# A two-block transformer layer on one core: POOL's matrix powers paced by tiles of the first feed-forward, products of ones at a boundary, and the output stored in quarters

## The chip, the cores and the metric

One core of a Trainium2 chip runs the whole program in one launch. The metric is the device time of the execution in microseconds (us); lower is better. The core has TensorE (PE, matrix products, with its weight loads as PEld), VectorE (DVE), ScalarE (ACT), GpSimd (POOL) and SyncE (SP, which here only issues transfers). The engines run their own instruction streams and meet at semaphores: `wait_ge(s, n)` holds an engine until semaphore `s` has reached `n`.

## The reference

256 tokens of width 1024 in float32 go through nine stages, each of which adds to the tokens `x`:

```python
x = x + 0.5 * ga1 * rms_norm(swiglu(modulate(rms_norm(x), sh1, sc1)))   # ffn 0
x = x + ga2 * rms_norm(mixer_1(modulate(rms_norm(x), sh2, sc2)))        # mix1: window attention + S5
x = x + 0.5 * ga3 * rms_norm(swiglu(modulate(rms_norm(x), sh3, sc3)))   # ffn 1
x = x + 0.5 * swiglu(rms_norm(x))                                       # ffn 2
x = x + mixer_2(rms_norm(x))                                            # mix2
x = x + 0.5 * swiglu(rms_norm(x))                                       # ffn 3, ffn 4
x = x + mixer_3(rms_norm(x))                                            # mix3
x = x + 0.5 * swiglu(rms_norm(x))                                       # ffn 5
out = rms_norm(x)
```

A feed-forward is `silu(h @ w_gate) * (h @ w_up)) @ w_down` with a hidden width of 2816, that is 22 tiles of 128. The modulation (`sh`, `sc`, `ga`) is `silu(c) @ w_ada + b_ada`, a product of one row with a 1024 x 9216 matrix. The S5 part of mix1 is a complex linear recurrence, `state = lam_bar * state + B_bar u`, `y = Re(C state)`. The kernel computes it in steps of four tokens and needs for that the powers of `lam_bar` multiplied into `B` and into `C`, turned into matrices for TensorE: the input map, the near map (what tokens of one step do to each other) and the output map. They depend on the parameters alone, so they are prepared during ffn 0.

## The kernel before

**Float32 by three products.** Every float32 operand of a large product is split into `hi` (rounded to the fast float32r form, by ScalarE) and `lo` (the rest, by VectorE), and `product3` (line 202) makes hi*hi + hi*lo + lo*hi: three passes through TensorE.

**The stream of panels.** All weights come as 458 panels of 128 x 1024. SP loads a panel into one of six `raw` buffers, ScalarE makes `w_hi` of it (`split_hi`, line 179), VectorE `w_lo` (`split_lo`, line 187), TensorE uses it and counts `panel_used`, which frees the buffer. So the splits can run at most six panels ahead of the products.

**A feed-forward.** Tile f has three panels: gate, up and down. `ffn_pe` (line 507) runs `up(f)` (gate and up products, 48 matmuls) and then `down(f - 1)` (12 wider ones), because between `up(f)` and `down(f)` ScalarE makes the silu, VectorE the hidden product (line 668, counted in `hidden_done`), ScalarE `f_hi` and VectorE `f_lo` (line 673). ScalarE and VectorE take, in their own programs, the three panel splits of group f, then the hidden work of tile f. `tiles(lo, hi)` is a loop over pairs of tiles: `tiles(0, 4)` is tiles 2 to 9.

**What else happens in ffn 0.** VectorE adds up the modulation: 2.5 additions of 128 x 1024 a tile (line 843), whose panels SP loads as well; at the end of the stage (tiles 18 to 21) TensorE sums the columns and the gate, and VectorE finishes them (lines 917 to 934). POOL works through `tables_pool` (line 1086): it issues three loads, computes four powers of B and four of C (`times_complex`, line 1072: six operations of 128 x 256 each), then two double angles, and then waits until `map_evacuated` has reached OUTPUT_MAP to build the table of rotations, `rot`, in the same memory as the powers of C. ScalarE widens and evacuates the maps: `input_wide_act` (needs `powers_ready` 1, after the B powers; eight activations), `near_map_act`, `input_map_act` twice, `output_map_act` (needs `powers_ready` 2; four activations). TensorE makes the products of the near map between its tiles and transposes the input map in two parts (`input_map_pe`, line 1183). All evacuations count one semaphore, `map_evacuated`, and every wait on it names a total. So the totals follow the order in which ScalarE does them:

```python
INPUT_WIDE, NEAR_MAP, INPUT_MAP, OUTPUT_MAP = 8, 9, 17, 21     # line 990
pe.wait_ge(map_evacuated, NEAR_MAP + max(n - 1, 0))            # line 1187, before transposes n = 0..7
pool.wait_ge(map_evacuated, OUTPUT_MAP)                        # line 1121, before the rotations
```

**Boundaries.** After a stage VectorE adds the four quarters of the result to X (a quarter is 128 tokens x 512 channels; quarters 0 and 2 come first into a "plain" stage), TensorE transposes X by 128 x 128 tiles (`turn_pe`, line 422), ScalarE and VectorE make `h_hi` and `h_lo` of them, and `norm_pe` (line 453) runs the first products of the next stage k tile by k tile. Stages from index PLAIN = 3 (ffn 2 is the first) scale by the norm only later. The boundary into ffn 2 is the only one into a plain stage behind a stage that is normed itself: VectorE multiplies the result by the gate row (line 764, counted in `times_gate`) before it adds (line 772), and there is no product left over for `last_quarter`. `keep_busy` (line 428) makes products of a matrix of ones, whose result nobody reads; some other boundaries have them.

**The end.** `norm_pool` makes the reciprocal root for each half of the tokens, VectorE multiplies each half (line 2830, 128 x 1024) and POOL stores each half (line 2774).

## Time and profile before

| | us |
|---|---|
| three runs: median (lowest to highest) | 1576.78 (1573.79 to 1578.28) |
| the profiled execution | 1575.49 |
| its span in the profile | 1573.7 |
| mean granted TensorE clock, as a share of full speed | 0.993 |
| ffn 0 on TensorE, from its first product to its last | 37.4 to 255.4 |
| boundary into ffn 2 | about 593 to 609 |
| last multiplication starts | 1566.3 |

All times of the trace are from the start of the span. A row of a time line is: start, duration, engine, line, operation, output and input by the program's names, count of instructions merged, and in brackets the idle time before it with what ended it. A row of the windows is: stretch, its length, then for each engine busy time and instruction count, then PEclk (the clock granted to TensorE; 1.00 is 2.4 GHz and 0.50 is 1.2 GHz), the busy share of the 16 DMA engines, and GB/s. Matmuls are pipelined, so neighbouring records overlap.

### The profile page before, as it was taken

The page shows a single profiled execution, that of the slowest core. Times are in us where ns is not written, and L with a number is a line of the kernel's source. Part 1 is how long each engine was busy: PE and PEld are TensorE (multiplying, and loading weights), DVE is VectorE, ACT ScalarE, POOL GpSimd, SP SyncE. Part 2 cuts the span into 40 slices and gives each one's busy share as a digit, 9 for nine tenths or more (in the row PEclk, how much of TensorE's full clock was granted, in tenths as well). Part 3 has the DMA queues.
Part 4 walks back from the last instruction along what each step waited for, and adds up shares of the span by engine and source line. Part 5 has one row for each costly group of instructions (what it writes and reads, how often), then busy time and mean ns, then how long its engine had stood idle before and what let it go on. Part 6 is the DMA issues. An engine that isn't in the chain of part 4 may idle for free.

```text
span 1573.7 us, 28410 instructions
## 1 busy us (share of the span) xinstructions
PE 1524.4 (97%) x10512; PEld 1401.8 (89%) x10512; DVE 1023.6 (65%) x1391; ACT 758.5 (48%) x1205; POOL 222.7 (14%) x255
## 2 busy tenths in 40 slices
PE   5989999999999998999999999999999999999997
PEld 5989999989988888999997899999999999899996
DVE  6998778766665456655567765556655569565554
ACT  2444645576456345444454344445444457454442
POOL 1596095311001011000000000000000000000000
PEclk9999999999999999999999999999999999999999
DMA  9888874236665455655543365554655544255551
GB/s 349 320 299 279 315 266 130 79 108 199 203 224 186 168 188 209 225 189 175 196 132 96 110 227 170 194 185 136 212 188 189 174 156 137 68 200 191 171 198 40
DMA packets 80563, 294.35 MB, mean 187 GB/s; under 512 B 9051, under 2 KB 9404, under 8 KB 79916
## 3 DMA queue, kind: packets, MB, share of 16 engines
q1 hardware_dynamic: 75728, 274.97, 50.8%
q0 software_dynamic: 3984, 16.21, 3.1%
q10 hardware_dynamic: 780, 2.18, 0.5%
q8 instruction: 50, 0.82, 0.2%
q14 instruction: 21, 0.17, 0.0%
HBM read 289.13 MB, written 3.15 MB: 186 GB/s over the span
## 4 chain that ended last, share of the span: by engine, by line
PE 84%; DVE 8%; ACT 3%; issue 2%; DMA 1%; POOL 1%; SPq 0%; DVEq 0%; ACTq 0%
PE bank L207 74%; DVE w_lo L191 3%; DVE arena L843 2%; PE bank L431 1%; PE bank L2033 1%; PE bank L2022 1%; PE bank L1273 1%; DMA arena<-ada 1%; PE bank L2409 1%; PE bank L2387 1%; ACT arena L308 1%; PE bank L424 1%; ACT w_hi L185 0%; PE bank L1259 0%; POOL stat L349 0%
## 5 line engine op out<-in xcount | busy, mean ns | idle before, releaser
L207 PE MATMUL bank<-h_hi,w_hi 128*128 128x256 f32 x2344 | 674.4, 288 | 5.8 <-DVE w_lo L191 4.4
L207 PE MATMUL bank<-h_lo,w_hi 128*128 128x256 f32 x2344 | 664.7, 284 | 0.0
L207 PE MATMUL bank<-h_hi,w_lo 128*128 128x256 f32 x2344 | 664.5, 283 | 0.0
L191 DVE TENSOR_TENSOR w_lo<-raw,w_hi 128x1024 fp32r<-128x1024 f32 x454 | 548.4, 1257 | 109.0 <-ACT w_hi L185 108.3
L185 ACT ACTIVATE w_hi<-raw 128x1024 fp32r<-128x1024 f32 x458 | 457.9, 1050 | 55.0 <-DMA raw<-panels 28.8
L207 PEld LDWEIGHTS bank<-h_hi,w_hi 128*128 128x128 f32 x2344 | 450.7, 192 | 21.0 <-issue 6.8
L207 PEld LDWEIGHTS bank<-h_lo,w_hi 128*128 128x128 f32 x2344 | 450.9, 192 | 5.7 <-issue 1.9
L207 PEld LDWEIGHTS bank<-h_hi,w_lo 128*128 128x128 f32 x2344 | 450.7, 192 | 0.0
L668 DVE TENSOR_TENSOR arena<-arena,bank 128x256 f32<-128x256 f32 x132 | 55.3, 419 | 253.7 <-PE bank L207 180.7
L207 PE MATMUL bank<-w_hi,f_hi 128*128 128x512 f32 x528 | 207.8, 394 | 1.6 <-DVE f_lo L673 1.4
L207 PE MATMUL bank<-w_hi,f_lo 128*128 128x512 f32 x528 | 206.9, 392 | 0.0
L207 PE MATMUL bank<-w_lo,f_hi 128*128 128x512 f32 x528 | 205.6, 389 | 0.0
L606 ACT ACTIVATE f_hi<-arena 128x256 fp32r<-128x256 f32 x132 | 55.1, 418 | 256.7 <-DVE arena L668 256.7
L348 POOL TENSOR_SCALAR stat<-stat 128x1 f32<-128x1 f32 x26 | 11.8, 455 | 995.3 <-ACT arena L308 994.5
L600 ACT ACTIVATE arena<-arena 128x256 f32<-128x256 f32 x88 | 36.8, 418 | 196.1 <-DVE arena L662 196.1
L207 PEld LDWEIGHTS bank<-w_lo,f_hi 128*128 128x128 f32 x528 | 99.2, 188 | 21.7
L207 PEld LDWEIGHTS bank<-w_hi,f_hi 128*128 128x128 f32 x528 | 99.6, 189 | 19.4 <-issue 1.6
L207 PEld LDWEIGHTS bank<-w_hi,f_lo 128*128 128x128 f32 x528 | 99.7, 189 | 15.8
L843 DVE SCALAR_TENSOR_TENSOR arena<-arena,stat 128x1024 f32<-128x1024 f32 x70 | 96.1, 1374 | 2.5 <-DMA arena<-ada 1.1
L673 DVE TENSOR_TENSOR f_lo<-arena,f_hi 128x256 fp32r<-128x256 f32 x132 | 60.9, 461 | 50.8 <-ACT f_hi L606 50.8
L604 ACT ACTIVATE arena<-bank 128x256 f32<-128x256 f32 x44 | 16.8, 382 | 134.1 <-PE bank L207 134.1
L662 DVE TENSOR_TENSOR arena<-bank,arena 128x256 f32<-128x256 f32 x88 | 37.2, 423 | 20.4 <-PE bank L207 20.4
(329 smaller groups left out, 1387.2 us busy)
## 6 DMA issues: line engine op xcount, KB each, us to landing
raw<-panels SPq DMA_DIRECT2D x458, 512.0 KB, 4.6
arena<-ada SPq DMA_DIRECT2D x64, 512.0 KB, 5.2
arena<-ada POOLq DMA_DIRECT2D x8, 512.0 KB, 3.9
arena<-rows POOLq DMA_DIRECT2D x4, 512.0 KB, 4.6
spectrum<-arena POOLq DMA_DIRECT2D x2, 1024.0 KB, 7.9
arena<-spectrum POOLq DMA_DIRECT2D x1, 2048.0 KB, 18.0
X<-x_in SPq DMA_DIRECT2D x1, 1024.0 KB, 6.7
arena<-decay ACTq DMA_DIRECT2D x2, 512.0 KB, 5.6
```

The costliest lines, as they stand in the source:

```text
L185: act.activation(w_hi[:, slot, :], raw[:, slot, :], ACT.Copy).then_inc(hi_ready, 1)
L191: dve.tensor_tensor(w_lo[:, slot, :], raw[:, slot, :], w_hi[:, slot, :].bitcast(F32), ALU.subtract).then_inc(lo_ready, 1)
L207: last = pe.matmul(out_ap, a, b, start=start and n == 0, stop=stop and n == 2)
L308: return act.activation(squares[:, q, :], source, ACT.Square, scale=D ** -0.5, accum_out=stat[:, at + q:at + q + 1])
L424: tr = pe.transpose(turned_out(n, k)[:, m * P:(m + 1) * P], X[:, m, k * P:(k + 1) * P], ident[:, :])
L600: act.activation(ffn_buf[:, f % 2, :], gate_buf[:, f % 2, :], ACT.Silu).then_inc(silu_done, 1)
L604: act.activation(ffn_buf[:, f % 2, :], gate_out(at, f), ACT.Silu).then_inc(silu_done, 1)
L606: act.activation(f_hi[:, f % 2, :], ffn_buf[:, 2 + f % 2, :], ACT.Copy).then_inc(f_hi_done, 1)
L662: dve.tensor_tensor(gate_buf[:, f % 2, :], gate_out(at, f), rstd_row[:, :], ALU.mult).then_inc(gate_scaled, 1)
L668: dve.tensor_tensor(ffn_buf[:, 2 + f % 2, :], ffn_buf[:, f % 2, :], up_out(at, f), ALU.mult).then_inc(hidden_done, 1)
L673: dve.tensor_tensor(f_lo[:, f % 2, :], ffn_buf[:, 2 + f % 2, :], f_hi[:, f % 2, :].bitcast(F32), ALU.subtract).then_inc(f_lo_done, 1)
L843: dve.scalar_tensor_tensor(out=dst, in0=src, scalar=c, in1=dst, op0=ALU.mult, op1=ALU.add).then_inc(ada_used, 1)
```

## The change

POOL computes the double angles before the powers, and every power but the first waits for a count of hidden products of ffn 0. ScalarE and TensorE take up the maps one pair of tiles later; the output map now comes ahead of the input map's evacuations, and the totals of `map_evacuated` are renumbered to fit. At the boundary into ffn 2 TensorE makes 14 products of ones before the transposes and, once all four gated quarters have been read, 5 more after the first eight transposes. The final multiplication is done in quarters, and SP stores three of them and ScalarE the last, in place of POOL's two halves.

```diff
@@ norm_pe
             if plain(n):
+                if n == PLAIN:
+                    keep_busy(pe, 7, 14)
                 for m in range(MT):
                     pe.wait_ge(x_done, added(n, 0, m))
                     for k in range(4):
                         turn_pe(pe, n, k, m)
+                if n == PLAIN:
+                    pe.wait_ge(times_gate, 4 * n)
+                    keep_busy(pe, 1, 5)
                 if n - 1 >= PLAIN:
                     last_quarter(pe, n - 1)
@@ ffn_pe, n == 0
-                tiles(0, 4)
+                tiles(0, 5)
                 near_map_first_pe(pe)
-                up(10, between=lambda: near_map_pe(pe, 0, 4))
+                up(12, between=lambda: near_map_pe(pe, 0, 4))
                 near_map_pe(pe, 4, 8)
-                down(9)
+                down(11)
                 near_map_pe(pe, 8, 12)
-                up(11, between=lambda: near_map_pe(pe, 12, STATE_TILES))
-                down(10)
-                tiles(5, 6)
+                up(13, between=lambda: near_map_pe(pe, 12, STATE_TILES))
+                down(12)
+                tiles(6, 7)
                 input_map_pe(pe, 0)
-                tiles(6, 7)
+                tiles(7, KT)
                 input_map_pe(pe, 1)
-                tiles(7, KT)
                 up(2 * KT + 2)
@@ ffn_act, n == 0
-                tiles(0, 3)
+                tiles(0, 4)
                 input_wide_act(act)
-                tiles(3, 5)
+                tiles(4, 6)
                 near_map_act(act)
-                tiles(5, 6)
+                tiles(6, 7)
+                output_map_act(act)
                 input_map_act(act, 0)
-                tiles(6, 7)
+                tiles(7, KT)
                 input_map_act(act, 1)
-                output_map_act(act)
-                tiles(7, FT // 2 - 2)
+                tiles(KT, FT // 2 - 2)
@@
-        INPUT_WIDE, NEAR_MAP, INPUT_MAP, OUTPUT_MAP = 8, 9, 17, 21
+        INPUT_WIDE, NEAR_MAP, OUTPUT_MAP, INPUT_MAP = 8, 9, 13, 21
@@ tables_pool: the block of the powers moves behind the double angles
             c1, s1 = double_angle(pr(LR), pr(LI))
             c1, s1 = double_angle(pr(YI), pr(EM1))
+            pool.wait_ge(ssm_loaded, 32)
+            raw_r, raw_i, c_r, c_i = [by_channel(ssm_raw[:, j, :]) for j in range(4)]
+            times_complex(pool, order, power_of(b_powers, 0, 3), power_of(b_powers, 1, 3), raw_r, raw_i,
+                          pr(CR), pr(CI))
+            for j in (2, 1, 0):
+                pool.wait_ge(hidden_done, 8 - 2 * j)
+                times_complex(pool, order, power_of(b_powers, 0, j), power_of(b_powers, 1, j),
+                              power_of(b_powers, 0, j + 1), power_of(b_powers, 1, j + 1), pr(DT), pr(XR))
+            pool.sem_inc(powers_ready, 1)
+            for i in range(STEP):
+                pool.wait_ge(hidden_done, (10, 12, 13, 14)[i])
+                source = (c_r, c_i) if i == 0 else (power_of(c_powers, 0, i - 1), power_of(c_powers, 1, i - 1))
+                times_complex(pool, order, power_of(c_powers, 0, i), power_of(c_powers, 1, i), *source,
+                              pr(DT), pr(XR))
+            pool.sem_inc(powers_ready, 1)
+
             pool.wait_ge(map_evacuated, OUTPUT_MAP)
@@ input_map_pe
-                pe.wait_ge(map_evacuated, NEAR_MAP + max(n - 1, 0))
+                pe.wait_ge(map_evacuated, OUTPUT_MAP + max(n - 1, 0))
@@ the end
+        def store_final(eng, q):
+            m, half = q // 2, quarter(q)
+            eng.wait_ge(final_done, q + 1)
+            eng.dma_start(out[m * P:(m + 1) * P, half], final[:, m, half]).then_inc(out_stored, 16)
@@ sync, behind the last load_panel
+            for q in (0, 1, 2):
+                store_final(sp, q)
+            sp.wait_ge(out_stored, 64)
@@ gpsimd
-            for m in range(MT):
-                pool.wait_ge(final_done, m + 1)
-                pool.dma_start(out[m * P:(m + 1) * P, :], final[:, m, :]).then_inc(out_stored, 16)
-            pool.wait_ge(out_stored, 32)
@@ scalar, behind the last norm_act
+            store_final(act, 3)
@@ vector
-            for m in range(MT):
+            for q in range(4):
+                m, half = q // 2, quarter(q)
                 dve.wait_ge(rstd_done, 2 * last + m + 1)
-                dve.scalar_tensor_tensor(out=final[:, m, :], in0=X[:, m, :],
-                                         scalar=stat[:, RS + m:RS + m + 1], in1=final_row[:, :],
+                dve.scalar_tensor_tensor(out=final[:, m, half], in0=X[:, m, half],
+                                         scalar=stat[:, RS + m:RS + m + 1], in1=final_row[:, half],
                                          op0=ALU.mult, op1=ALU.mult).then_inc(final_done, 1)
```

## Rows read from the trace of the kernel before

**Rows 1.** The page: shares of the chain that ended last, by engine.
```profile
PE 84%; DVE 8%; ACT 3%; issue 2%; DMA 1%; POOL 1%; SPq 0%; DVEq 0%; ACTq 0%
```

**Rows 2.** Groups of VectorE, 65 to 135 us: shapes, count | busy us, mean ns | idle before.
```profile
L191 DVE TENSOR_TENSOR w_lo<-raw,w_hi 128x1024 fp32r<-128x1024 f32 x21 | 33.5, 1647 | 2.0 <-ACT w_hi L185 2.0
L843 DVE SCALAR_TENSOR_TENSOR arena<-arena,stat 128x1024 f32<-128x1024 f32 x19 | 28.6, 1506 | 0.1
L673 DVE TENSOR_TENSOR f_lo<-arena,f_hi 128x256 fp32r<-128x256 f32 x7 | 6.4, 911 | 0.0
```

**Rows 3.** The same groups of VectorE, 146 to 196 us.
```profile
L843 DVE SCALAR_TENSOR_TENSOR arena<-arena,stat 128x1024 f32<-128x1024 f32 x13 | 16.6, 1279 | 0.1
L191 DVE TENSOR_TENSOR w_lo<-raw,w_hi 128x1024 fp32r<-128x1024 f32 x12 | 14.0, 1218 | 4.2 <-ACT w_hi L185 4.2
...
L673 DVE TENSOR_TENSOR f_lo<-arena,f_hi 128x256 fp32r<-128x256 f32 x5 | 2.1, 417 | 0.0
```

**Rows 4.** Time line of POOL: first and last of 48 power operations, then the rotations' start.
```profile
65.73 0.89 POOL L1075 TENSOR_TENSOR arena<-arena,par 128x256 f32<-128x256 f32 x1 [2.60 <-DMA arena<-skip]
...
133.02 1.60 POOL L1080 TENSOR_TENSOR arena<-arena 128x256 f32<-128x256 f32 x1
...
196.84 0.96 POOL L938 MEMSET arena<- 128x1024 f32 x1 [52.22 <-ACT arena L1149]
```

**Rows 5.** The chain that ended last, one undisturbed feed-forward tile: start, duration, count.
```profile
499.31 8.50 PE bank L207 x60
```

**Rows 6.** Time line of TensorE around the gap in feed-forward 0.
```profile
114.51 0.39 PE L207 MATMUL bank<-w_lo,f_hi 128*128 128x512 f32 x1
118.13 0.39 PE L207 MATMUL bank<-h_hi,w_hi 128*128 128x256 f32 x1 [3.23 <-DVE w_lo L191]
```

**Rows 7.** Windows of 2 us before and after that gap.
```profile
96.00:98.00 2.00, 0.84 (x6) 0.67 (x6) 2.00 (x2) 0.00 (x0) 1.84 (x3) 1.00 0.80 219
...
118.00:120.00 2.00, 1.87 (x12) 1.87 (x13) 2.00 (x3) 0.98 (x2) 2.00 (x2) 0.76 0.60 172
120.00:122.00 2.00, 2.00 (x11) 2.00 (x11) 2.00 (x3) 0.43 (x2) 1.92 (x3) 0.50 0.80 248
```

**Rows 8.** Time line of ScalarE: input widening, f_hi of tile 15, output widening.
```profile
110.01 5.86 ACT L1149 ACTIVATE arena<-arena,C 128x1024 f32<-128x1024 f32 x8
...
187.98 0.42 ACT L606 ACTIVATE f_hi<-arena 128x256 fp32r<-128x256 f32 x1 [0.65 <-DVE arena L668]
...
192.46 4.26 ACT L1149 ACTIVATE arena<-arena,C 128x1024 f32<-128x1024 f32 x4
```

**Rows 9.** Time line of TensorE: the input map's second transposes, behind tile 15.
```profile
189.50 1.03 PE L1189 MATMUL bank<-ident,arena 128*128 128x128 f32 x8
```

**Rows 10.** Windows at the boundary into ffn 2, and one 230 us earlier.
```profile
597.00:600.00 3.00, 1.99 (x9) 1.99 (x10) 3.00 (x6) 2.45 (x8) 0.00 (x0) 0.50 0.03 5
600.00:603.00 3.00, 3.00 (x16) 3.00 (x16) 1.23 (x3) 0.95 (x2) 0.00 (x0) 0.50 0.42 143
...
368.00:370.00 2.00, 2.00 (x17) 1.88 (x17) 2.00 (x5) 1.39 (x5) 1.37 (x3) 1.00 0.00 0
```

**Rows 11.** Time line of TensorE at the boundary into ffn 2.
```profile
594.61 0.66 PE L424 MATMUL bank<-ident,X 128*128 128x128 f32 x4 [1.48 <-DVE X L772]
596.30 0.65 PE L424 MATMUL bank<-ident,X 128*128 128x128 f32 x4 [1.03 <-DVE X L772]
598.01 0.58 PE L207 MATMUL bank<-h_hi,w_hi 128*128 128x256 f32 x1 [1.06 <-DVE h_lo L407]
```

**Rows 12.** Time line of TensorE: 24 calls of `keep_busy` at the boundary into ffn 1.
```profile
368.50 5.52 PE L431 MATMUL bank<-ones 128*128 128x128 f32 x48
```

**Rows 13.** Time line of the end: last multiplication and POOL's issue of its store.
```profile
1566.28 1.28 DVE L2830 SCALAR_TENSOR_TENSOR arena<-X,stat,arena 128x1024 f32<-128x1024 f32 x1 [0.84 <-POOL stat L349]
1567.87 0.53 POOL L2774 DMA_DIRECT2D out<-arena  x1 [1.04 <-DVE arena L2830]
```

**Rows 14.** Transfers by issue: engine, count, KB each, us from issue to landing.
```profile
out<-arena POOLq DMA_DIRECT2D x2, 512.0 KB, 2.9
```

More of the change, by code:

```diff
@@ L1094, in tables_pool @@
             order(pool.tensor_copy(pr(XR), pr(LI)))
-            pool.wait_ge(ssm_loaded, 32)
-            raw_r, raw_i, c_r, c_i = [by_channel(ssm_raw[:, j, :]) for j in range(4)]
-            times_complex(pool, order, power_of(b_powers, 0, 3), power_of(b_powers, 1, 3), raw_r, raw_i,
-                          pr(CR), pr(CI))
-            for j in (2, 1, 0):
-                times_complex(pool, order, power_of(b_powers, 0, j), power_of(b_powers, 1, j),
-                              power_of(b_powers, 0, j + 1), power_of(b_powers, 1, j + 1), pr(DT), pr(XR))
-            pool.sem_inc(powers_ready, 1)
-            for i in range(STEP):
-                source = (c_r, c_i) if i == 0 else (power_of(c_powers, 0, i - 1), power_of(c_powers, 1, i - 1))
-                times_complex(pool, order, power_of(c_powers, 0, i), power_of(c_powers, 1, i), *source,
-                              pr(DT), pr(XR))
-            pool.sem_inc(powers_ready, 1)
             c1, s1 = pr(COS), pr(SIN)
```

## The prediction

> **What bounds the kernel now.** I read the shares of the page first: TensorE carries 84% of the chain that ended last, VectorE 8% and ScalarE 3% [rows 1]. So nearly every microsecond is a product, and the change can only touch the few places where the products stop. Next I read the time lines of the engines around the three edits. Three places matter.
>
> First, tiles 3 to 9 of feed-forward 0 (of 22). A tile of a feed-forward takes TensorE 8.5 us when it waits for nothing [rows 5]. Per tile VectorE has three panel subtractions, a hidden product, f_lo and 2.5 additions of the modulation sums. Where POOL is computing its powers these cost 1.65, 1.51 and 0.91 us [rows 2], where it rests 1.22, 1.28 and 0.42 us [rows 3]. With the overlap of neighbouring records taken off, a tile is 9.6 us for VectorE with POOL at work (3 x 1.6 + 0.4 + 0.9 + 2.5 x 1.4) and 7.2 without. POOL's powers run without a break from 65.7 to 134.6 us [rows 4], so there VectorE, at 9.6 us against TensorE's 8.5, sets the pace and falls behind. When ScalarE then widens the input map for 5.9 us [rows 8], nothing is left in store, and TensorE stands from 114.9 to 118.1 us [rows 6], released by a w_lo. Right after that gap its granted clock falls to the lower of the two levels, 1.2 GHz: 0.76 and 0.50 of 2.4 GHz in the next windows of 2 us [rows 7].
>
> Second, the boundary into the third feed-forward. TensorE ends its products at 593.1 (1.48 us of idle time before 594.61), makes transposes at 594.6 and 596.3 and gets its first product at 598.0 [rows 11]; from 597 to past 603 the clock stands at 0.50 [rows 10].
>
> Third, the end: the last multiplication starts at 1566.28, POOL issues its store at 1567.87 [rows 13], it lands 2.9 us after its issue [rows 14], and 2.9 us more pass until the span ends at 1573.7.
>
> **Part 1, the paced powers.** The double angles move ahead of the powers: 134.6 to 144.6 us is 10.0 us of POOL [rows 4], so powers start at about 73.2 instead of 65.7. One power is 68.9 / 8 = 8.6 us [rows 4]. The new waits hold the second to fourth b power to tiles 3, 5 and 7, the c powers to tiles 9, 11, 12 and 13. up(9) starts at 118.1 now [rows 6] and, with what is found below, at about 113; at 8.5 us a tile [rows 5] this puts the hidden products of tiles 3, 5 and 7 at about 70, 88 and 105.5, tile 9's at 123, and tile 15's at about 180, the near map's products being in between. So b runs at 73 to 82, 82 to 91 (tile 3 is long done), 91 to 100, then a rest until tile 7 at about 105.5, 106 to 115, and c at 123 to 131, 141 to 150, 151 to 160, 162 to 171. Everything queued behind them on POOL waits too: the two increments that ScalarE needs. The first comes at 115, wanted after tile 9; the second at 171, wanted after tile 15. Neither is late.
>
> VectorE is then slowed about half of the time between 66 and 123 instead of all of it. It loses 2.4 us a tile under POOL, so 23 us over 9.6 tiles become about 14, and it was TensorE's 8.5 that it had to meet: the panels are no longer late at tiles 6 to 8. What goes at most is the gap of 3.2 us [rows 6], the loss at the low clock, 2 x 0.24 + 2 x 0.50 = 1.5 us and 0.2 until it is back [rows 7], the 1.2 us without a product at 96 to 98 us (0.84 busy of 2.00 [rows 7]) and 0.3 of gaps too small for a row: 6.4 us. What is late next is the same widening of the maps, now after tile 9. Between the end of up(9) and the start of up(11) TensorE has 11.3 us of work (down, up, down: 2.75 + 5.75 + 2.75, which are 8.5 us and a third of it more [rows 5]); the path through tile 9's hidden product, its f_hi, 5.9 us of widening, one w_hi and one contended w_lo takes 9.3 us and VectorE's own lateness. That lateness I get as about 3.4 us (it loses 1.1 us a tile under POOL, and wins 1.3 in between), so 1.4 us of a gap stay. Part: 6.4 - 1.4 = **-5.0 us**; ends -6.4 and -1.4 (VectorE as late as now).
>
> **The wait that the change adds.** In the new numbering the evacuations are 8 input wide, 9 near map, 13 output map, 21 input map, and `input_map_pe` starts with a wait for 13: the transposes of the input map stand behind all four widenings of the output map, for no reason of data. Today those widenings come after everything (192.46) and nobody on TensorE waits for them. In the changed order ScalarE is through with a tile's f_hi 1.1 us before TensorE reaches the transposes (187.98 + 0.42 = 188.4 against 189.5 [rows 8, 9]) and then widens for 4.3 us [rows 8]: 188.4 + 4.3 - 189.5 = 3.2 us in which TensorE stands, and behind it everything else in its program. ScalarE's near map, the contention of the last c power and a late hidden product can make it 4.3. I take **+3.5**; ends 0 (were the vector engines' panels late there anyway) and +4.3. A gap of 3.2 us has cost the clock in this very stage [rows 6, 7], so I add its **+1.7**; ends 0 and +3.1 (half of the 6.2 us at 0.50 of the boundary [rows 10]). The Trainium skill ("TensorE: Matmul & The Clock Gate", Part 4) says that transposes do not count as activity for the clock; the 16 transposes of the map would then lengthen the quiet stretch, and the trace agrees so far as eight transposes at 594.6 and 596.3 did not hold the clock [rows 10, 11]. By that rule the fall is certain, by row 6 alone it is likely.
>
> The rotation, which waits for the output map, starts about 11 us earlier (186 instead of 196.84 [rows 4]) and ends at 237 instead of 248. Its longest operations then lie on VectorE's sums for the second gate (229 to 235 today) and no longer on the last two tiles. I take **+0.3**; ends -1.0 and +1.8 (the sums slowed as in rows 2). Part 1 together: -5.0 + 3.5 + 1.7 + 0.3 = **+0.5 us**.
>
> **Part 2, products of ones.** 24 such calls are 48 instructions in 5.5 us [rows 12], 0.115 us each. 14 calls: 28 x 0.115 = 3.2 us, from 593.1 to 596.3. The first transposes could have gone at 594.6; they go at 596.3 and end at 596.7, and the second ones, ready at 596.3, are 0.4 us late; the path runs through these. 5 calls, 1.15 us, fill 597.2 to 598.3 while h_hi and h_lo are made. The new wait for the gated quarters holds nothing: VectorE gates the last of them before the addition that releases the second transposes. The products of the first k tiles, 598.0 to 603.4, then run at 2.4 GHz instead of 1.2: 5.4 / 2 = 2.7 us less. The squares and the row of reciprocals follow the last of these tiles, so they move along. -2.7 + 0.4 and 0.1 for a step of the h_lo chain that becomes the slower one = **-2.2 us**; ends -2.7 and +0.4 (the clock falls all the same).
>
> **Part 3, the store.** The last quarter is ready when the last half is today, plus 0.1 us for the start of one more instruction. Its issue need not wait 0.3 us for POOL (1566.28 + 1.28 against 1567.87 [rows 13]), and it moves 256 KB instead of 512, which saves between nothing and half of 2.9 us [rows 14]; I take 0.6, in the lower half, since it still has 128 rows to place. Three of four stores go behind SP's last panel load and one behind ScalarE's last square; nothing is queued behind them. -0.3 - 0.6 + 0.1 = -0.8, and a little of the 0.53 us that POOL's issue itself takes [rows 13]: **-0.9**; ends +0.1 and -1.8. The Trainium skill ("DMA: Bandwidth & Descriptors", Latency and other measured facts) gives a first byte after 0.6 us on the hardware queues and 1 us on POOL's; by that the part would be 0.4 us more of a gain. No row here shows it.
>
> **Sum**: +0.5 - 2.2 - 0.9 = -2.6 us. The profiled execution took 1575.49 us (span 1573.7 and 1.8 around it), 1.3 below the median of the three runs, 1576.78. 1575.5 - 2.6 = 1572.9; against the median 1574.2, which I give, as the runs after will be judged so. About 0.3% (4.7 us) can be told from no change.
>
> **The rivals.**
> A. The map wait costs no clock and VectorE really gets ahead: part 1 is -6.4 + 3.2 + 0 - 0 = -3.2, the sum -6.3, 1570.5 us. For it: the fall needs a gap, and a ScalarE that is early makes it shorter. Against: the gap before the fall today is as long [rows 6]. 0.25.
> B. The products of ones do not hold the clock at the boundary: part 2 is +0.4, the sum 0.0, 1576.8 us. For it: they are the same 128 columns wide as the transposes. Against: at the boundary before, 24 calls [rows 12] hold 1.00 [rows 10]. 0.12.
> C, slower. VectorE stays the bound of tiles 3 to 9, so that only 1.4 us of the early loss go, and the transposes of the input map wait 4.3 us and lose 3.1 us of clock, with the gate's sums slowed by 1.8: -1.4 + 4.3 + 3.1 + 1.8 = +7.8, less 3.1 of the other parts, +4.7 us, 1581.5. It decides from a lateness of 5.3 us of the hidden product of tile 9 after up(9), where the gap is again 3.2 us. For it: three b powers still run without a break. Against: the rests before tiles 7 and 9. 0.10.
> D. The edit does nothing at that place, since the powers' contention is only moved: early gain 3 instead of 5, sum -0.6, 1576.2. 0.08.
>
> **How the numbers follow.** The forecast, 0.45, reaches from 1571.5 to 1577. Faster by over 0.3% are A and a small part of the forecast: 0.32. Slower is C and nothing else: 0.10. The rest, 0.58, is within 0.3%. The range takes in A and B and stops short of C: 1569.0 to 1579.0.
>
> **What would show it.** Right: in the stretch from 75 to 123 us no TensorE gap over 2 us and the clock at 1.00; powers in six bursts; a TensorE gap of 3 to 4.5 us before L1189's first transposes, released by ScalarE's L1149, and a clock of 0.5 in the 5 us after it; the boundary near 595 at 1.00 with the row product about 2 us sooner after the last down product; the last store landing within 2.5 us. Wrong: a gap of the old size at the widening (C), no gap at the transposes (A), a 0.50 near 600 (B).

## The result, and the profile after

| | before | after |
|---|---|---|
| median of 6 runs on one chip, us | 1575.34 (1573.03 to 1578.28) | 1566.87 (1566.01 to 1568.16) |
| profiled execution, us | 1575.49 | 1566.55 |
| its span, us | 1573.7 | 1563.9 |
| mean granted clock | 0.993 | 0.997 |

The changed kernel takes 0.9946 of the time of the kernel before, 95% interval 0.9932 to 0.9960: 8.5 us less. The forecast was 2.6 us less and its range ended at 1569.0, so the result lies outside it, on the fast side. Of the 7.3 us between the forecast of 1574.2 and the 1566.87 measured, 1.4 are the base: the forecast started from the median of three runs of the kernel before, 1576.78, and the median of six is 1575.34. The other 5.9 are the change.

The page's chain of the changed kernel has more of TensorE and less of VectorE than [rows 1]:

```profile
PE 87%; DVE 6%; ACT 3%; issue 2%; DMA 1%; POOL 1%; SPq 0%; DVEq 0%; POOLq 0%; ACTq 0%
```

**Feed-forward 0, first part.** Groups of VectorE by shape, 65 to 135 us, changed kernel (count | busy us, mean ns | idle before), against [rows 2]:

```profile
L191 DVE TENSOR_TENSOR w_lo<-raw,w_hi 128x1024 fp32r<-128x1024 f32 x25 | 34.9, 1446 | 2.5 <-ACT w_hi L185 2.5
L847 DVE SCALAR_TENSOR_TENSOR arena<-arena,stat 128x1024 f32<-128x1024 f32 x20 | 28.3, 1417 | 0.1
L677 DVE TENSOR_TENSOR f_lo<-arena,f_hi 128x256 fp32r<-128x256 f32 x8 | 4.4, 553 | 0.0
```

VectorE makes 25 panels in the stretch instead of 21, and one takes 1446 ns instead of 1647. The time line of GpSimd shows why. The powers come in bursts: the last b power starts at 104.02, the first two c powers at 120.36 and 138.08, with 6 to 10 us of rest before each (and 4.3 us before the last c power at 161), released by VectorE's hidden product:

```profile
104.02 1.87 POOL L1079 TENSOR_TENSOR arena<-arena,par 128x256 f32<-128x256 f32 x1 [6.50 <-DVE arena L672]
...
120.36 1.94 POOL L1079 TENSOR_TENSOR arena<-arena,par 128x256 f32<-128x256 f32 x1 [6.43 <-DVE arena L672]
...
138.08 1.86 POOL L1079 TENSOR_TENSOR arena<-arena,par 128x256 f32<-128x256 f32 x1 [10.30 <-DVE arena L672]
```

In TensorE's time line the gap of 3.23 us of [rows 6] is gone. up(9) starts at 111.67, 0.23 us behind the product before it, as at every tile, and at the widening, which is now a tile pair later, there is a hole of 0.25 us beyond that (128.44 to 128.92):

```profile
111.44 0.39 PE L207 MATMUL bank<-w_lo,f_hi 128*128 128x512 f32 x1
111.67 0.28 PE L207 MATMUL bank<-h_hi,w_hi 128*128 128x256 f32 x1
...
128.44 0.39 PE L207 MATMUL bank<-w_lo,f_hi 128*128 128x512 f32 x1
128.92 0.39 PE L207 MATMUL bank<-h_hi,w_hi 128*128 128x256 f32 x1
```

**The wait that the change adds.** Time line of all engines at the first input map, changed kernel, against [rows 8, 9]:

```profile
178.91 0.42 ACT L610 ACTIVATE f_hi<-arena 128x256 fp32r<-128x256 f32 x1 [1.54 <-DVE arena L672]
...
179.23 4.25 ACT L1156 ACTIVATE arena<-arena,C 128x1024 f32<-128x1024 f32 x4
179.30 0.39 PE L207 MATMUL bank<-w_lo,f_hi 128*128 128x512 f32 x1
...
183.54 3.47 PE L1196 MATMUL bank<-ident,arena 128*128 128x128 f32 x16 [3.85 <-ACT arena L1156]
```

TensorE is through at 179.7 and stands for 3.85 us until ScalarE has widened the output map (L1156). Windows of 2 us: the clock falls, as forecast:

```profile
182.00:184.00 2.00, 0.46 (x2) 0.47 (x3) 0.92 (x1) 1.48 (x2) 0.46 (x1) 0.78 1.04 401
184.00:186.00 2.00, 2.00 (x11) 1.76 (x10) 0.00 (x0) 1.06 (x2) 1.63 (x7) 0.50 1.02 395
186.00:188.00 2.00, 2.00 (x17) 1.87 (x16) 0.00 (x0) 1.64 (x4) 1.61 (x8) 0.86 0.69 277
```

When it rises again stands in two shorter windows and the time line of TensorE: at 1.00 for most of 186.50 to 186.75, while the first product behind the transposes starts at 186.76.

```profile
186.00:186.50 0.50, 0.50 (x5) 0.37 (x4) 0.00 (x0) 0.14 (x2) 0.42 (x2) 0.50 0.96 393
186.50:186.75 0.25, 0.25 (x4) 0.25 (x3) 0.00 (x0) 0.25 (x1) 0.17 (x2) 0.90 1.05 427
...
186.76 0.36 PE L207 MATMUL bank<-h_hi,w_hi 128*128 128x256 f32 x1
```

**The boundary into feed-forward 2.** Windows of 3 us, changed kernel: the clock stays at 1.00 where [rows 10] had 0.50.

```profile
593.00:596.00 3.00, 3.00 (x28) 3.00 (x27) 3.00 (x7) 2.98 (x9) 0.00 (x0) 1.00 0.00 0
596.00:599.00 3.00, 3.00 (x28) 3.00 (x27) 2.06 (x5) 1.89 (x5) 0.00 (x0) 1.00 0.32 101
```

**The end.** Time line and transfers of the changed kernel, against [rows 13, 14]:

```profile
1558.49 2.59 SPq L2712 DMA_DIRECT2D out<-arena  x3
...
1559.96 1.42 DVE L2844 SCALAR_TENSOR_TENSOR arena<-X,stat,arena 128x512 f32<-128x512 f32 x2 [0.84 <-POOL stat L349]
1561.41 0.36 ACTq L2712 DMA_DIRECT2D out<-arena  x1
```

The last quarter is issued at 1561.41 and lands 2.1 us later, at 1563.5; the span ends at 1563.9, 0.4 us behind. Before, the last landing was at 1570.8 and the span went on for 2.9 us.

**Where the time went, by milestones.** From the traces of the two kernels and of the twelve experiments below (time lines of TensorE) five stretches can be cut:

- S0: start of the span to the first product of up(3) (the expectations below say the third tile);
- S1: from there to the last down product ahead of the near map (its start, as for all that follow), less the 17.0 us of the two tiles that come earlier in the new order;
- S2: from the last down product ahead of the first input map to the last product of the up behind it;
- S3: from up(3) to the first product on diag behind feed-forward 0, at the boundary into mix1 (261.45 in before, 257.76 in after), S1 and S2 being part of it;
- S4: from there to the first product on diag at the boundary into feed-forward 2 (608.27 of before, 601.87 of after), called the row product below;
- T: from the last such product (1381.53 and 1375.08) to the end of the span.

| us | S0 | S1 | S2 | S3 | S4 | T |
|---|---|---|---|---|---|---|
| before | 62.0 | 66.0 | 8.1 | 199.4 | 346.8 | 192.2 |
| after | 60.7 | 59.6 | 13.2 | 197.1 | 344.1 | 188.8 |

Between the row product at 608.27 and the one at 1381.53 nothing changes: 773.26 before, 773.21 after, 773.2 to 773.3 in every run. S0 is no part of the change. Kernels that are the same up to there had 60.2 to 63.7 us in it, with the first product at 35.8 to 39.7 us; the table's 1.3 us is such a difference.

### The profile page after: what moved, and what is told of

Same layout as the page of the kernel before. It is cut to its first block, busy times and chain, and to the rows that moved or that the text cites. A ratio compares the mean times of both kernels' runs of the same rounds, so it can differ in the third digit from the quotient of the medians.

```text
span 1563.9 us, 28493 instructions
## 1 busy us (share of the span) xinstructions
PE 1524.2 (97%) x10550; PEld 1403.9 (90%) x10550; DVE 1019.3 (65%) x1393; ACT 758.7 (49%) x1205; POOL 217.1 (14%) x253
## 4 chain that ended last, share of the span: by engine, by line
PE 87%; DVE 6%; ACT 3%; issue 2%; DMA 1%; POOL 1%; SPq 0%; DVEq 0%; POOLq 0%; ACTq 0%
PE bank L207 76%; DVE w_lo L191 2%; PE bank L431 2%; DVE arena L847 1%; PE bank L2040 1%; PE bank L2029 1%; PE bank L1280 1%; PE bank L2416 1%; PE bank L2394 1%; PE bank L424 1%; ACT arena L1156 1%; PE bank L1266 0%; DMA raw<-panels 0%; PE bank L1592 0%; DMA arena<-ada 0%
```

## The experiments

The theory behind them: the three parts act at three places and do not meet, part 1 pays by pacing and loses most of it again at the input map, and part 3 pays by its queue (experiments 5 to 7 correct the last). The rivals are in the expectations. Each interval is of the ratio to the kernel before on the same chip.

**1 to 3. Each part alone on the kernel before**

```diff
 store_only:   + store_final(sp, q) for q in (0, 1, 2); sp.wait_ge(out_stored, 64); store_final(act, 3); VectorE in quarters
 ones_only:    + keep_busy(pe, 7, 14) and keep_busy(pe, 1, 5) where n == PLAIN, with the wait for times_gate
 powers_only:  + the POOL block, the tiles and the numbering of the maps as changed
```

> The kernel before, with the final store in quarters from SyncE and ScalarE and nothing else of the change. The prediction's terms give 0.9 us less. The reading of the two traces gives more: after VectorE's last product the changed kernel's span goes on for 2.5 us where the kernel before took some 6, so this run alone should be 2.5 to 3.4 us faster, its end lying about 0.4 us behind the last landing. If instead the shorter tail came from the state in which the earlier parts left the queues, this run gains under 1 us and keeps a 2.9 us stretch behind its last landing.

> The kernel before, with the products of ones at the third feed-forward's boundary and nothing else of the change. The prediction's term is 2.2 us less, the traces of the two kernels differ by 2.6 us over that boundary: 2.2 to 2.6 us faster, with the granted clock at 1.00 from 597 to 603 us. The rival in which the products don't hold the clock gives 0 to 0.4 us slower, with 0.50 in that stretch.

> The kernel before, with the order of the matrix powers and of the maps as changed, without the ones and without the new store. The prediction's terms give 0.5 us slower. The two traces differ by 3.8 us by the second feed-forward's first up, of which 1.35 us is there at the third tile of the first feed-forward, before anything of the change has run: if that share belongs to the run and not to the kernel, this run is 1.9 to 3 us faster than before; if it is a true effect of the changed kernel, 3.8 us. TensorE is to wait 3.9 us at the transposes of the first input map in either case.

| | median, us | before, us | ratio, interval | S1 | S2 | S3 | S4 | T |
|---|---|---|---|---|---|---|---|---|
| store_only | 1572.18 | 1574.71 | 0.9982 (0.9971 to 0.9994) | 67.0 | 8.1 | 200.4 | 347.0 | 188.8 |
| ones_only | 1574.01 | 1574.71 | 0.9995 (0.9986 to 1.0004) | 64.5 | 8.1 | 197.9 | 344.2 | 192.2 |
| powers_only | 1572.15 | 1574.71 | 0.9985 (0.9977 to 0.9994) | 59.6 | 13.7 | 197.5 | 345.6 | 192.1 |

The store alone takes 3.4 us off T and 2.5 us off the median. The powers take about 2 us off S3 and 2.6 off the median, so the 1.35 us that the changed kernel was ahead at up(3) was not theirs. The ones take 2.6 us off S4, but their median is only 0.7 us lower, and its interval reaches from 2.2 us faster to 0.6 slower. Experiment 9 goes back to that. The three medians add up to 5.8 us, the whole change to 8.5; the four intervals together are wide enough for the difference, and the stretches of the traces do add up (S3, S4 and T: 8.0 us in the three runs together, 8.4 in the changed kernel, each against the trace of before).

Part of it lies outside the span. In every run with a span on record of the kernel before, and of the eight variants without both groups of ones, the device time is 1.8 us above the span (at most 1.85). In the five kernels with both groups (ones_only, the changed kernel, map_order, no_pacing, old_places) it is 2.3 to 2.9 us in 28 of 46 runs. By the spans ones_only is 1.7 us faster (means 1571.2 against 1572.9) and not 0.7. Where the added time comes from, no run shows: fourteen_only and five_only, with one group each, have 1.8 us in all of their four runs.

In powers_only, which has no ones, S4 is itself 1.2 us shorter than before: the clock was at the lower level for a shorter time. Windows of powers_only:

```profile
594.00:597.00 3.00, 2.04 (x9) 2.04 (x10) 3.00 (x6) 2.40 (x8) 0.00 (x0) 0.64 0.02 5
597.00:600.00 3.00, 3.00 (x23) 3.00 (x22) 1.18 (x3) 1.43 (x3) 0.00 (x0) 0.80 0.48 154
```

**4. The wait at the transposes taken away (changed kernel)**

```diff
+                input_map_act(act, 0)
                 output_map_act(act)
-                input_map_act(act, 0)
...
-        INPUT_WIDE, NEAR_MAP, OUTPUT_MAP, INPUT_MAP = 8, 9, 13, 21
+        INPUT_WIDE, NEAR_MAP, OUTPUT_MAP, INPUT_MAP = 8, 9, 17, 21
...
-                pe.wait_ge(map_evacuated, OUTPUT_MAP + max(n - 1, 0))
+                pe.wait_ge(map_evacuated, NEAR_MAP + max(n - 1, 0) + (4 if n > 5 else 0))
```

> The changed kernel, with ScalarE evacuating the first input map ahead of the output map instead of behind it, so that TensorE's transposes do not wait for the output map. The wait of 3.9 us at the transposes should go. If that wait is a loss on the path, this kernel is 3.5 to 5 us faster than the changed one (about 1562.5 us); the rotation on GpSimd then starts some 10 us later, and if the gate of the state ladder is what is late next, 1 to 3 us of it come back at the 20th tile. If the wait was cover for ScalarE and VectorE all along, the gain is under 1 us.

1562.73 us, ratio 0.9929 (0.9913 to 0.9944): by the medians 4.1 us faster than the changed kernel and 12.0 less than the kernel before in the same comparison (by the two ratios 2.7 us faster than the changed kernel; one of its six runs took 1566.52). S2 is 8.1 us as before the change, S3 192.7. Time lines of TensorE and ScalarE in that kernel:

```profile
180.33 1.03 PE L1196 MATMUL bank<-ident,arena 128*128 128x128 f32 x8
...
180.97 1.09 ACT L1205 ACTIVATE arena<-bank 128x512 f32<-128x512 f32 x2 [0.82 <-PE bank L1196]
...
183.29 4.26 ACT L1156 ACTIVATE arena<-arena,C 128x1024 f32<-128x1024 f32 x4
```

The widening (L1156) now lies behind the evacuations, beside TensorE's products. S3 fell by 4.4 us where S2 fell by 5.0: some 0.6 us come back at the second gate, whose up starts 26.9 us after the up behind the second transposes instead of 26.3. The wait was a loss on the path. This version is clearly faster than the kernel before; its interval and that of the changed kernel (0.9932 to 0.9960) overlap, and that it beats this one too rests on the stretch that the edit concerns, 4.4 us shorter in the traces.

**5 to 7. What of the store pays (kernel before)**

```diff
 sp_halves:      two halves of 512 KB, issued and waited for by SyncE
 sp_waits:       - pool.wait_ge(out_stored, 32)
                 + sp.wait_ge(out_stored, 32)
 pool_quarters:  VectorE in quarters; pool: 4 x store_final, pool.wait_ge(out_stored, 64)
```

> The kernel before, its final store still in two halves of 512 KB, but issued and waited for by SyncE instead of GpSimd; VectorE unchanged. In the trace of before the span goes on for 2.9 us behind the landing of the last half, in the two kernels that store from SyncE and ScalarE for 0.4 us. If that stretch and the slower landing (2.9 against 2.1 us) belong to the queue, moving the queue alone saves most of what the quarters from SyncE saved in the span (3.3 us): 2.5 to 3.3 us. If the quarters are what saves, by shorter landings and an earlier start, this run saves under 0.5 us.

> The kernel before, GpSimd still issuing the two halves of the final store, but SyncE waiting for their landing instead of GpSimd. If the 2.9 us behind the last landing are GpSimd's slow waking from its wait, they go here, and the run is 2.5 us faster. If they lie in the DMA path of GpSimd's queue (its completion, or the queue's closing), this run takes the same time as before, within 0.3 us.

> The kernel before, the final products and stores in quarters as in the change, but all four stores issued and waited for by GpSimd. If the quarters bring the gain, 0.5 to 0.9 us less than before; if the queue alone does, within 0.3 us of before, or up to 0.5 us slower for two more issues of 0.58 us each on GpSimd.

The transfers by issue (KB each, us from issue to landing) of sp_halves, pool_quarters and store_only, in this order:

```profile
out<-arena SPq DMA_DIRECT2D x2, 512.0 KB, 2.6
```

```profile
out<-arena POOLq DMA_DIRECT2D x4, 256.0 KB, 2.8
```

```profile
out<-arena SPq DMA_DIRECT2D x3, 256.0 KB, 2.1
```

| | issuer, size | who waits | T | last issue | landing | end of span behind the landing | ratio, interval |
|---|---|---|---|---|---|---|---|
| before | POOL, 512 KB | POOL | 192.16 | 1567.87 | 2.9 | 2.9 | |
| sp_waits | POOL, 512 KB | SP | 190.73 | 1569.61 | 2.9 | 1.5 | 0.9990 (0.9980 to 1.0000) |
| pool_quarters | POOL, 256 KB | POOL | 192.74 | about 1567.9 | 3.1 (median 2.8) | 3.1 | 0.9998 (0.9989 to 1.0007) |
| sp_halves | SP, 512 KB | SP | 189.10 | about 1565.8 | 2.6 | 0.4 | 0.9970 (0.9958 to 0.9982) |
| store_only | SP and ACT, 256 KB | SP | 188.79 | 1567.31 | 2.1 | 0.4 | 0.9982 (0.9971 to 0.9994) |

The medians of experiments 5 to 7 are 1570.97, 1573.67 and 1575.67 us, against 1575.06 for the kernel before. What pays is that GpSimd no longer stores, not the quarters: halves from SyncE save 3.1 of the 3.4 us of T, and quarters from GpSimd save nothing (T 0.6 us longer). Neither of the two expectations for sp_waits holds: letting SyncE wait takes 1.4 us off the stretch behind the landing, and 1.5 us of it stay.

The traces say what the stretch is. Each engine's program ends with a DRAIN, recorded on L85, the `with` line of the whole program. From 1555 us on (count, duration in ns as least/median/most, start in us) in before, then in sp_waits, then GpSimd's and SyncE's in sp_halves:

```profile
L85 POOLq DRAIN  x1: 2514/2514/2514, 1571.0 to 1571.0; - x1
```

```profile
L85 POOLq DRAIN  x1: 4195/4195/4195, 1569.6 to 1569.6; - x1
```

```profile
L85 POOLq DRAIN  x1: 2983/2983/2983, 1563.8 to 1563.8; - x1
...
L85 SPq DRAIN  x1: 7/7/7, 1568.6 to 1568.6; - x1
```

GpSimd's DRAIN takes 2.5 us after the stores of before have landed and 3.0 us in sp_halves, where GpSimd has none; SyncE's takes 0.007 us. In before it can start only when GpSimd's wait for the landing (1570.8) is over, and it ends at 1573.5, 0.2 us ahead of the end of the span. In sp_halves it starts at 1563.8, beside the stores, and is over at 1566.8, ahead of the last landing at 1568.4; in the changed kernel it runs from 1559.3 to 1562.3. In sp_waits it starts at the issue of the last half, lasts 4.2 us and ends 1.3 us behind the landing. So the span ends shortly after the later of two things, the landing or the end of GpSimd's DRAIN, and GpSimd's part in the store decides when the DRAIN can start. Why it takes 4.2 us in sp_waits and not 3.0 is open; 0.6 us of it lie beside the issue.

**8. The pacing alone taken away (changed kernel)**

```diff
-                pool.wait_ge(hidden_done, 8 - 2 * j)
...
-                pool.wait_ge(hidden_done, (10, 12, 13, 14)[i])
```

> The changed kernel without the waits of GpSimd's powers for the hidden tiles; the maps stay where the change puts them. The first tiles' stretch, from the third tile's first product to the near map, took 66.0, 67.0 and 64.5 us in the three traces with the old order, and 59.6 us (for as many tiles) in all three with the new one. If the pacing is the cause, this kernel falls back: GpSimd's powers then run in one burst beside the widening of w_lo on VectorE, TensorE waits for it again, and the run is 4 to 6 us slower than the changed kernel (about 1571 to 1573 us). If the cause is only that the maps start two tiles later and the widening with them, it stays within 1.5 us of the changed kernel (1566.9 us).

1574.39 us, ratio 0.9992 (0.9983 to 1.0001): 7.5 us slower than the changed kernel, more than expected. S1 is 67.7 us against 59.6. The groups of VectorE and the time line of TensorE of that kernel show the old picture again, a panel at 1629 ns and a gap at the widening, only two tiles later:

```profile
L191 DVE TENSOR_TENSOR w_lo<-raw,w_hi 128x1024 fp32r<-128x1024 f32 x22 | 34.8, 1629 | 1.9 <-ACT w_hi L185 1.9
```

```profile
113.93 0.39 PE L207 MATMUL bank<-h_hi,w_hi 128*128 128x256 f32 x1 [1.22 <-DVE w_lo L191]
...
135.20 0.58 PE L207 MATMUL bank<-h_hi,w_hi 128*128 128x256 f32 x1 [3.69 <-DVE w_lo L191]
```

Without the pacing nothing is left of the early gain, though the double angles still come first. Later maps without it are worse than the old order (S1 67.7 against 64.5 to 67.0 in the six runs with the old order).

**9 to 11. Which products of ones hold the clock (changed kernel)**

```diff
 no_ones:        - keep_busy(pe, 7, 14)    - keep_busy(pe, 1, 5), with its wait
 fourteen_only:                            - keep_busy(pe, 1, 5), with its wait
 five_only:      - keep_busy(pe, 7, 14)
```

> The changed kernel without the products of ones at the third feed-forward's boundary. Alone on the kernel before, the ones brought 2.6 us in the profiled execution but only 0.7 us in the medians (interval of the ratio 0.9986 to 1.0004). If their worth is the 2.6 us that the half clock costs there in nearly every run, this kernel is 2.2 to 2.6 us slower than the changed one (1566.9 us), with 0.50 of the clock for 4 to 5 us between 590 and 603 us. If the clock falls there in only some of the runs, or for a shorter time (3.3 us in the run with the paced powers alone), it is 0.7 to 1.5 us slower, with a wider spread.

> The changed kernel with the first products of ones (7 times 14, ahead of the transposes) and without the five behind them. If the clock at this boundary is lost by the idle time ahead of the transposes, this is as fast as the changed kernel within 0.5 us. If the last five are needed as well, the clock is 0.50 behind the transposes and it is as slow as without any ones, 2 to 2.6 us more.

> The changed kernel with the five products of ones behind the transposes alone, without those ahead of them. If what matters is the idle time ahead of the transposes, it is as slow as without any ones, 2 to 2.6 us more than the changed kernel. If the last gap before the products of the feed-forward decides, it is within 0.5 us of the changed kernel.

| | median, us | ratio, interval | S4 |
|---|---|---|---|
| no_ones | 1568.75 | 0.9965 (0.9951 to 0.9978) | 347.0 |
| five_only | 1568.49 | 0.9959 (0.9943 to 0.9974) | 346.7 |
| fourteen_only | 1566.66 | 0.9948 (0.9933 to 0.9963) | 344.1 |
| all (the changed kernel) | 1566.87 | 0.9946 (0.9932 to 0.9960) | 344.1 |

Windows of no_ones, then of fourteen_only:

```profile
594.00:597.00 3.00, 2.76 (x13) 2.76 (x14) 2.63 (x6) 2.16 (x7) 0.00 (x0) 0.50 0.02 5
597.00:600.00 3.00, 3.00 (x16) 3.00 (x16) 0.83 (x2) 0.71 (x2) 0.00 (x0) 0.50 0.56 175
```

```profile
594.00:597.00 3.00, 2.12 (x18) 1.88 (x18) 3.00 (x7) 1.98 (x6) 0.00 (x0) 1.00 0.00 0
597.00:600.00 3.00, 3.00 (x29) 3.00 (x27) 2.52 (x5) 2.13 (x7) 0.00 (x0) 1.00 0.17 20
```

The fourteen calls ahead of the transposes do it all. The five behind them bring nothing beside those, and alone they come at a clock that is already 0.50. Over all traces, S4 is 344.1 to 344.2 us in the six with the fourteen calls; without the fourteen it is 346.4 to 347.0 in seven and 345.6 in powers_only. The worth of the ones is thus 2.6 us of the span in most executions and less in some. The medians say 1.9 (no_ones against all, from two comparisons), 2.1 (no_ones against fourteen_only, in one comparison) and 0.7 (ones_only, whose interval still holds 1.9). The intervals of no_ones and of the kernels with the fourteen calls overlap, so that which calls do it rests on S4 and the clock in the windows. By the spans, which leave out the time that both groups together add outside it, the ones are worth 2.4 us (no_ones 1567.1 against 1564.7, means).

**12. The pacing without the new places of the maps**

```diff
 every map at its old tile and in its old order:
+                tiles(0, 3)
                 input_wide_act(act)
+                tiles(3, 5)
                 near_map_act(act)
...
+        INPUT_WIDE, NEAR_MAP, INPUT_MAP, OUTPUT_MAP = 8, 9, 17, 21
 (ones, store and the POOL block as in the changed kernel)
```

> The changed kernel with every map at its old tile and in its old order (the near map behind tile 9, both input maps before the output map); of the first part only GpSimd's powers are changed, paced by the hidden tiles. If the pacing alone is what gains and the shift of the maps only brings the wait of 3.9 us at the transposes, this kernel is as fast as the one with the maps' order changed back (1562.7 us), with 0.5 us more at the first boundary where the rotation on GpSimd ends late as before: 1562.5 to 1563.5 us. If the maps need their two tiles of delay (the b powers not ready when ScalarE comes to the widening, or VectorE late behind it), TensorE waits near the eighth and ninth tile, 2 to 5 us, and this kernel takes 1565 to 1568 us.

1574.27 us, ratio 0.9999 (0.9990 to 1.0009): the rival of that expectation, and 6 us slower than the top of its range. S1 is 69.0 us. ScalarE comes to the widening of the input map and waits 7.11 us for the last b power, which GpSimd has begun only at 104.54, held by the hidden tiles; VectorE then waits 9.74 us for a w_hi and TensorE 7.72 us for a w_lo. Time lines of GpSimd, ScalarE, VectorE and TensorE, then a window:

```profile
104.54 1.87 POOL L1080 TENSOR_TENSOR arena<-arena,par 128x256 f32<-128x256 f32 x1 [6.49 <-DVE arena L673]
...
111.95 5.86 ACT L1157 ACTIVATE arena<-arena,C 128x1024 f32<-128x1024 f32 x8 [7.11 <-POOLq L1121]
...
118.79 3.49 DVE L191 TENSOR_TENSOR w_lo<-raw,w_hi 128x1024 fp32r<-128x1024 f32 x3 [9.74 <-ACT w_hi L185]
...
120.07 0.58 PE L207 MATMUL bank<-h_hi,w_hi 128*128 128x256 f32 x1 [7.72 <-DVE w_lo L191]
```

```profile
120.00:122.00 2.00, 1.93 (x9) 1.93 (x10) 2.00 (x3) 0.92 (x2) 0.00 (x0) 0.50 0.32 63
```

The two halves of part 1 need each other: pacing at the old places loses as much as later places without pacing. A pacing one hidden pair looser, or a widening one pair later alone, was not tried.

## Why the prediction was wrong

**The step that failed** is in part 3: the prediction noted that 2.9 us more pass between the last landing and the end of the span, and put nothing on them in its sum. In the runs 2.5 of these 2.9 us go, since they are GpSimd's closing DRAIN. Three more terms had the right place and the wrong size, the early gain (1.4 us), the gate and the rotation (1.5, and the other sign) and the ones (0.4), all in the same direction as the store; the wait for the output map was off by 0.3 the other way. By the prediction's own terms (measured values are from the stretches above, as means over the six traces with the old order, before among them, and the five with part 1 as changed):

| term | forecast | measured | from |
|---|---|---|---|
| early gain | -5.0 | -6.4 | S1 66.0 to 59.6 |
| wait for the output map, with its clock | +3.5 + 1.7 | +5.5 | S2 8.1 to 13.6 (13.2 to 14.5) |
| gate and rotation | +0.3 | -1.2 | S3 less S1 and S2, 125.3 to 124.1 |
| ones | -2.2 | -2.6 | S4 |
| store | -0.9 | -3.4 | T |
| sum | -2.6 | -8.1 | -8.5 in the runs |

**The store was the largest miss**, 2.5 us, and the only term clearly outside its own ends (+0.1 and -1.8). The prediction had read that "2.9 us more pass until the span ends" and then summed only what lies before the landing: issue, start and size of the transfer. It took the stretch behind the landing for a constant of the program, without a reason. 1.4 us of T go when SyncE waits in GpSimd's place, 1.6 more when SyncE issues too. With the store as forecast the measured terms make -5.6 us, which is 1571.2 from the forecast's base, inside the range. The issue is as forecast (0.03 us behind VectorE's last product instead of 0.3). Quarters shorten the landing from 2.6 to 2.1 us (sp_halves and store_only), about the 0.6 of the forecast, but T by only 0.3. The Trainium skill ("DMA: Bandwidth & Descriptors", Latency and other measured facts) has a faster first byte on the hardware queues by 0.4 us; the landings agree in sign, 2.6 against 2.9 us for 512 KB, but that is the small part of it.

**The early gain.** The mis-sized term is VectorE's lateness at tile 9. It was put at 3.4 us, which left 1.4 us of a gap at the widening. In the changed kernel the hidden product of tile 9 is at 119.88 and up(9) ends at 117.4, a lateness of 2.5, and 0.25 us of a gap is left. With the gap gone the whole of the forecast's end of -6.4 came, whose working was right to 0.1 us. Rival C, which needed a lateness of 5.3, was far off. The order of the bursts (three powers without a break, then rests before 104, 120 and 138) is as forecast, within 3 us.

**The wait.** Right, and to its size: 3.2 to 4.3 us of standing were expected and 3.85 is in the row; released by the widening, ending at 183.5, clock at 0.50 behind it. It costs 5.0 to 6.4 us with its clock; taking it away gives 4.1 (medians) and 4.4 (S3), or 2.7 by the two ratios. The Trainium skill's rule that transposes do not count for the clock ("TensorE: Matmul & The Clock Gate", Part 4) was weighed there. The trace of the changed kernel does not agree: from the fall of the clock to its rise at about 186.55 TensorE ran nothing but the sixteen transposes, and the first product came at 186.76. The measurement decides: the transposes did count here. The fall has a standing of 3.85 us ahead of it, like the gap of [rows 6, 7], and needs no such rule. Rival A, with no clock cost, was right only in VectorE's lead.

**The gate and the rotation.** Forecast +0.3 with ends -1.0 and +1.8. It came out at the lower end, 0.2 us beyond it. The rotation's last record ends about 231 instead of 249, so VectorE's last sums and the boundary's row no longer lie beside it: from the gate's up to the last down product it is 19.9 us in all traces with part 1, 20.3 in four of the six without; from there to the row product 5.6 against 5.9 to 6.0. old_places, with the powers of the change but the output map and so the rotation at its old late place, has 20.3 and 6.0 again: the difference goes with the rotation's place, not with the powers. These two make some 0.7 of the 1.2 us; for the rest no run shows a cause.

**The ones.** Right in kind, and rival B is out. The price that the forecast put on the late transposes (0.4) is not to be seen: from the last down product to the first up product it is 5.3 us in before and after. The five calls, which it placed beside the making of h_hi and h_lo, bring nothing.

Rival D (contention only moved, an early gain of 3) is out: S1 fell by 6.4 us, and rose by 8.1 again without the pacing. 0.4 us between the sum and the runs stay open.

## What to carry to other kernels

When a span goes on behind its last landing, look at what each engine does last before calling it a constant: here GpSimd's closing DRAIN of 2.5 to 3.0 us waited for the store, and giving the store to SyncE, alone or with ScalarE, let it run earlier and ended this program 3 us sooner. Pacing one engine's side work helps only if what waits for that work is moved back by as much, and every place that it is moved past has to be read for a new wait: here one line's order on ScalarE gave back 4 us of a gain of 6. Calls that hold the clock went ahead of the idle stretch here; behind it they already ran at the lower level.

## What the hardware showed unexpectedly

- With GpSimd issuing and waiting, the span ended 2.9 us behind the last landing, with GpSimd issuing and SyncE waiting 1.5, with SyncE doing both 0.4. GpSimd's DRAIN at the end of its program took 2.5 to 3.0 us with no store under way, SyncE's 0.007.
- Sixteen float32 transposes alone, with no other product, brought the granted clock back from 0.50 to 1.00 (changed kernel, 183.54 to 186.76).
- The same operation of a power on GpSimd takes 1.61 us while VectorE works and 0.75 while it rests (changed kernel, time line of GpSimd): the slowing goes both ways.

```profile
109.08 1.61 POOL L1082 TENSOR_TENSOR arena<-arena 128x256 f32<-128x256 f32 x1
...
125.51 0.75 POOL L1082 TENSOR_TENSOR arena<-arena 128x256 f32<-128x256 f32 x1
```

- Products of ones behind the idle stretch did not lift the clock while they ran: in five_only ten of them took 2.34 us, in the changed kernel, at full clock, 1.28.

```profile
595.16 2.34 PE L431 MATMUL bank<-ones 128*128 128x128 f32 x10
```

```profile
593.15 1.28 PE L431 MATMUL bank<-ones 128*128 128x128 f32 x10
```

- The time outside the span is not a constant: 1.8 us in the runs of nine kernels, up to 2.9 us in the five that have both groups of ones.
- S1 took 64.5 to 67.0 us in the old order, and 59.6 or 59.7 in each of the six traces with the new one.
